# All loops written out, and both heads of a level moved together in the recurrence's inverse

## Chip, core and metric

The kernel runs on one core of one Trainium2 chip. The metric is the time of one execution in device microseconds; the kernel before takes 2701.41 us (median of 3 runs, 2699.93 to 2706.42). The engines are named as in the profile: PE (TensorE; PEld is its weight loads, PEq its sequencer), DVE (VectorE), ACT (ScalarE), POOL (GpSimd) and SP (SyncE, here only loads). A name with a q behind it (DVEq, ACTq, PEldq) stands for an engine's sequencer rows: waits, register operations, branches.

## The reference

Two decoder layers over 512 tokens of width 1024, each between two half-step SwiGLU FFNs. Layer 0 is RWKV-7 time mixing with 16 heads of 64, layer 1 is sparse attention over shared keys and values.

```python
for l in range(DEPTH):                      # DEPTH = 2
    x = x + 0.5 * swiglu(rmsnorm(x, norm_ffn1[l]), ffn1_w_gate[l], ffn1_w_up[l], ffn1_w_down[l])
    h = rmsnorm(x, norm_mix[l])
    if l < N_A:  x = x + rwkv7_time_mix(h, ...)       # layer 0
    else:        x = x + nsa_attention(h, shared, ...)  # layer 1
    x = x + 0.5 * swiglu(rmsnorm(x, norm_ffn2[l]), ffn2_w_gate[l], ffn2_w_up[l], ffn2_w_down[l])
    if l == N_A - 1:  shared = nsa_shared_kv(x, ...)
# inside rwkv7_time_mix, for every head and token:
    sa = jnp.einsum('bhij,bhj->bhi', state, -kk_t)
    state = (state * w_t[:, :, None, :] + sa[..., None] * (kk_t * a_t)[:, :, None, :]
             + v_t[..., :, None] * k_t[..., None, :])
    y = jnp.einsum('bhij,bhj->bhi', state, r_t)
```

## The kernel before

The program is a row of stages, one after another, each with its own set of semaphores and a barrier between: a transpose of x, FFN, mix_project (the RWKV projections), recurrence, project_add, FFN, shared_kv, FFN, queries, attention, project_add, FFN, and a transpose back. In every stage each engine has its own instruction list, and semaphores order them (`wait_ge` before an instruction, `then_inc` behind it). The order within a list is the order in which the code is written.

**The projections.** Float32 products are made in three passes of rounded high and low parts (`three_passes`, L146 to L152). SP loads a weight unit of 128x1024 into one of four slots, DVE splits it (`split_unit`: a CAST on L141, a subtraction on L143), PE multiplies it. In `ffn` the gate and up units of a group run in a hardware loop (`Fori`, L258, L264, L287, L331, L334, L362, L380) with four units in its body; the down units are written out. `mix_project` has such a loop for each of its projections k and v on every engine (L451) and for r on all but SP and DVE; beside the units of k, DVE makes two mixed tiles per unit (L488, L492). `attention` is a loop of two iterations (L1691, L1789, L1843, L1950) whose body holds 44 written-out steps on PE, ACT and DVE. In a loop every wait whose value depends on the iteration needs a register, which its own small instruction sets (in attention they all have line L1655).

**The recurrence** (L613 on) is written out already: it walks through 8 pairs of heads, two heads h = 0, 1 at a time, in chunks of 64 tokens. Each pair needs the inverse of a unit triangular 64x64 matrix for each of 8 chunks and both heads. It is doubled up in five levels (`LEVELS`). The factor and its transpose of head h lie in `xx[h]` (called `x[h]` and `xt[h]`). One level is, for each head: 8 small matmuls `parts @ x` into PSUM bank 6 + h ("the g matmuls", L842), a copy to `g[h]` by ACT (L1008, waits for semaphore g_mm), 16 small matmuls of `g[h]` and `xt[h]` into bank 2h ("the x matmuls", L853 and L856, wait for g), and an addition into `xx[h]` by DVE (L1166, waits for x_mm); the next level's g matmuls wait for that addition (semaphore x). The last level updates only the transpose (L1168). A small float32 matmul shows as two records in the trace. Between the g and the x matmuls of levels 0 to 3 PE does a piece of the next pair's preparation (`prepare`, parts 0 to 3); in the last pair there is none. The core of a level on DVE and on ACT:

```python
for h in range(2):                                   # DVE, L1162
    at(dve, p, "x_mm", 2 * level + h + 1)
    TT(both, bank[:, 2 * h], both, ALU.add).then_inc(s["x"], 1)
for h in range(2):                                   # ACT, L1006
    at(act, p, "g_mm", 2 * part + h + 1)
    A(g[h]..., bank[:, 6 + h, 0:NT * C], ACT.Copy).then_inc(s["g"], 1)
```

After the levels PE applies the inverse (L865, "the au matmuls", 64x128 each), ACT copies both heads (L1014), and a chain of states over the chunks follows (L901, L926, L1182).

Of the kernel before, what the change touches and what calls it, by code (L numbers as in the profile page):

```python
# [13 lines left out]
P = 128  # L14
# [164 lines left out]
class Norm:  # L179
# [37 lines left out]
    def tensor(self, pe):  # L217

        if self.first:
# [5 lines left out]
            "act32", "silu", "sq", "sq_sum", "ready"] + NORM_SEMS  # L225
# [6 lines left out]
def ffn(core, tag, x_gain, w_gate, w_up, w_down, ahead):  # L232
# [6 lines left out]
    with ExitStack() as ctx:  # L239
# [14 lines left out]
        def _(sp):  # L254
            unit = 0
            for f0, nf in groups:
                skip = 1 if f0 == 0 else 0
                with sp.Fori(0, nf // 2 - skip) as i:  # L258
# [5 lines left out]
                with sp.Fori(0, ND // 4) as i:  # L264
# [8 lines left out]
        def _(dve):  # L273
# [11 lines left out]
            for f0, nf in groups:  # L285

                with dve.Fori(0, nf // 2) as i:  # L287
# [22 lines left out]
        def _(pe):  # L310
# [4 lines left out]
            for f0, nf in groups:  # L315
# [13 lines left out]
                if f0 == 0:  # L329
                    gate_up(0, True)  # L330
                    with pe.Fori(0, nf // 2 - 1) as i:  # L331
                        gate_up(i + 1, False)
                else:
                    with pe.Fori(0, nf // 2) as i:  # L334
                        gate_up(i, False)
# [21 lines left out]
        def _(act):  # L357
# [3 lines left out]
            for f0, nf in groups:  # L361
                with act.Fori(0, nf // 2) as i:  # L362
                    for j in range(2):
# [5 lines left out]
                        act.sem_inc(s["ready"], 1)  # L369
# [5 lines left out]
        def _(pool):  # L375
# [4 lines left out]
            for f0, nf in groups:  # L380
                with pool.Fori(0, nf // 2) as i:
                    for j in range(2):
# [6 lines left out]
                        pool.sem_inc(s["ready"], 1)  # L389
# [14 lines left out]
            "dx", "mix32", "mix_hi", "mix_lo", "out", "st0", "st1", "st2", "st3", "ready", "pad"]  # L404


def mix_project(core, tag, rkv, lora):
# [21 lines left out]
    with ExitStack() as ctx:  # L429
# [13 lines left out]
        def units_of(eng, name, body, unrolled=False):  # L443
# [6 lines left out]
            elif name in MAIN:  # L450
                with eng.Fori(0, n // 4) as i:  # L451
# [23 lines left out]
        def _(dve):  # L475
            dve.sem_inc(s["w_ready"], SLOTS)
            dve.sem_inc(s["ready"], 1)

# [38 lines left out]
        def _(act):  # L517
# [5 lines left out]
            def round_tile(name, m, slot, d):  # L523
                act.wait_ge(s["mix32"], m + 1)
                act.wait_ge(s["ready"], 1)
# [31 lines left out]
        def _(pool):  # L557
# [4 lines left out]
            def low_tile(name, m, slot, d):  # L562
                pool.wait_ge(s["mix_hi"], m + 5)
                pool.wait_ge(s["ready"], 1)
# [43 lines left out]
    "score": 3, "bl": 2, "kl": 2, "nm": 2, "part": 2, "x_init": 4, "lakv": 1, "aw": 1, "g_mm": 10, "g": 10,  # L608
    "x_mm": 10, "x": 10, "au_mm": 2, "au": 2, "rp_mm": 1, "rp": 1, "f_mm": 1, "f": 1, "z_mm": 1, "z": 1, "within": 1,
# [14 lines left out]
def recurrence(core, tag, rkv, lora, yhi, ylo):  # L624
# [16 lines left out]
    with ExitStack() as ctx:  # L641
# [101 lines left out]
        def _(pe):  # L743
# [48 lines left out]
            def step(p, slot, first, last):  # L792
# [34 lines left out]
                for level in range(len(LEVELS)):  # L827
                    over = level == len(LEVELS) - 1
                    for h in range(2):
# [8 lines left out]
                        else:  # L838
                            at(pe, p, "x", 2 * (level - 1) + h + 1)
# [4 lines left out]
                        mm.then_inc(s["g_mm"], 1)  # L844
                        if level == 0 and h == 0:
                            lak_v()
                    if not last and level < 4:
                        prepare(p + 1, 1 - slot, level)
                    for h in range(2):
                        at(pe, p, "g", 2 * level + h + 1)  # L850
# [7 lines left out]
                        mm.then_inc(s["x_mm"], 1)  # L858

                at(pe, p, "aw", 1)  # L860
                for h in range(2):
                    at(pe, p, "x", 8 + h + 1)
# [79 lines left out]
        def _(act):  # L942
# [55 lines left out]
            def step(p, slot, first, last):  # L998
# [1158 lines left out]
```

## Time and profile before

| | |
|---|---|
| median of 3 runs | 2701.41 us |
| the profiled execution's own time | 2708.74 us |
| its span, first to last instruction | 2706.9 us |
| PE busy, DVE busy | 2434.5 us (90%), 1606.1 us (59%) |
| ACT busy, POOL busy | 634.9 us (23%), 563.5 us (21%) |
| mean granted PE clock | 0.948 |
| instruction fetches by PE (queue q8) | 113 packets, 1.85 MB |

The busy times are sums over stages with different limits, so they are to be read by stage. The stages begin, in us from the span's start, at 17 (FFN), 393 (mix), 598 (recurrence), 999 (project_add), 1052 (FFN), 1422 (shared_kv), 1541 (FFN), 1912 (queries), 2000 (attention), 2273 (project_add) and 2326 (FFN, to 2697).

### The profile page before, as it was taken

What the parts mean: (1) busy time and instruction counts of PE and PEld (TensorE: products, weight loads), DVE (VectorE), ACT (ScalarE), POOL (GpSimd) and SP (SyncE); (2) the same over time, 40 slices, a digit from 0 to 9 for tenths busy, and PEclk for the clock granted to TensorE, in tenths of its full rate; (3) what the DMA queues carried; (4) which work ended last, traced back from release to release, by engine and by line L of the source; (5) the groups of instructions that cost most, each with busy time, mean ns of one, the idle gap of its engine ahead of it and who ended that gap; (6) DMA issues with size and microseconds to landing.
All of it is one profiled execution on the core that took longest, in us unless ns stands there. A gap on an engine that the chain in (4) does not pass through costs nothing. (4 is left out here: it accounts for less than half of the span.)

```text
span 2706.9 us, 44357 instructions
## 1 busy us (share of the span) xinstructions
PE 2434.5 (90%) x16952; PEld 1977.2 (73%) x16952; DVE 1606.1 (59%) x2182; ACT 634.9 (23%) x1246; POOL 563.5 (21%) x382
## 2 busy tenths in 40 slices
PE   7999977987888869999999699999849898999998
PEld 6888865765666657888877588888638687788887
DVE  6646569945666545656556465656536565565654
ACT  3100012223545322101012310101435453210001
POOL 3212135421212102302030021213111300221213
PEclk9999997998999979999999799999969899999999
DMA  4333222430000012333325333332351101333331
GB/s 133 103 94 101 82 74 71 128 110 29 16 30 16 17 33 78 96 99 101 94 78 163 106 101 94 93 99 73 113 130 37 37 2 32 94 103 91 103 87 66
DMA packets 375943, 216.95 MB, mean 80 GB/s; under 512 B 18880, under 2 KB 359808, under 8 KB 375776
## 3 DMA queue, kind: packets, MB, share of 16 engines
q1 hardware_dynamic: 367648, 198.83, 26.0%
q10 hardware_dynamic: 8128, 15.83, 1.6%
q8 instruction: 113, 1.85, 0.3%
q14 instruction: 54, 0.44, 0.1%
HBM read 198.73 MB, written 15.89 MB: 79 GB/s over the span
## 5 line engine op out<-in xcount | busy, mean ns | idle before, releaser
L143 DVE TENSOR_TENSOR w_lo_ffn<-w_raw,w_hi_ffn 128x1024 fp32r<-128x1024 f32 x272 | 508.7, 1870 | 9.4
L387 POOL TENSOR_TENSOR act_ffn<-gated_ffn,usc_ffn 128x512 f32<-128x512 f32 x88 | 128.1, 1456 | 1007.4 <-ACT gated_ffn L367 1007.4
L367 ACT ACTIVATE gated_ffn<-gsc_ffn 128x512 f32<-128x512 f32 x88 | 55.8, 634 | 1010.4 <-DVE gsc_ffn L292 1010.4
L150 PE MATMUL p_gate_ffn<-hhi_ffn,w_hi_ffn 128*128 128x512 f32 x704 | 278.2, 395 | 7.6 <-DVE hlo_ffn L205 7.6
L150 PE MATMUL p_up_ffn<-hhi_ffn,w_hi_ffn 128*128 128x512 f32 x704 | 274.6, 390 | 2.9 <-DVE w_lo_ffn L143 2.9
L151 PE MATMUL p_gate_ffn<-hlo_ffn,w_hi_ffn 128*128 128x512 f32 x704 | 277.2, 394 | 0.0
L150 PE MATMUL p_down_ffn<-ahi_ffn,w_hi_ffn 128*128 128x512 f32 x704 | 274.9, 390 | 2.4 <-DVE x_res L303 2.4
L152 PE MATMUL p_gate_ffn<-hhi_ffn,w_lo_ffn 128*128 128x512 f32 x704 | 276.9, 393 | 0.0
L292 DVE TENSOR_TENSOR gsc_ffn<-p_gate_ffn,rstd_ffn 128x512 f32<-128x512 f32 x88 | 60.9, 692 | 363.6 <-PE p_up_ffn L152 363.0
L151 PE MATMUL p_up_ffn<-hlo_ffn,w_hi_ffn 128*128 128x512 f32 x704 | 274.6, 390 | 0.0
L152 PE MATMUL p_up_ffn<-hhi_ffn,w_lo_ffn 128*128 128x512 f32 x704 | 274.5, 390 | 0.0
L152 PE MATMUL p_down_ffn<-ahi_ffn,w_lo_ffn 128*128 128x512 f32 x704 | 273.9, 389 | 0.0
L151 PE MATMUL p_down_ffn<-alo_ffn,w_hi_ffn 128*128 128x512 f32 x704 | 273.9, 389 | 0.0
L141 DVE CAST w_hi_ffn<-w_raw 128x1024 fp32r<-128x1024 f32 x272 | 191.1, 702 | 29.5 <-PEq L311 29.5
L303 DVE SCALAR_TENSOR_TENSOR x_res<-p_down_ffn,x_res 128x512 f32<-128x512 f32 x96 | 66.3, 690 | 204.1 <-PE p_down_ffn L152 204.1
L390 POOL TENSOR_TENSOR alo_ffn<-act_ffn,ahi_ffn 128x512 f32 x88 | 150.6, 1712 | 98.7 <-ACT ahi_ffn L370 98.7
L150 PEld LDWEIGHTS p_gate_ffn<-hhi_ffn,w_hi_ffn 128*128 128x128 f32 x704 | 134.3, 191 | 40.7 <-DVE w_lo_ffn L143 12.3
L150 PEld LDWEIGHTS p_down_ffn<-ahi_ffn,w_hi_ffn 128*128 128x128 f32 x704 | 132.1, 188 | 34.1 <-issue 7.1
L150 PEld LDWEIGHTS p_up_ffn<-hhi_ffn,w_hi_ffn 128*128 128x128 f32 x704 | 132.6, 188 | 31.0 <-DVE w_lo_ffn L143 3.4
L151 PEld LDWEIGHTS p_gate_ffn<-hlo_ffn,w_hi_ffn 128*128 128x128 f32 x704 | 134.1, 191 | 28.3 <-issue 0.2
L152 PEld LDWEIGHTS p_gate_ffn<-hhi_ffn,w_lo_ffn 128*128 128x128 f32 x704 | 134.1, 191 | 28.2
L152 PEld LDWEIGHTS p_up_ffn<-hhi_ffn,w_lo_ffn 128*128 128x128 f32 x704 | 132.5, 188 | 27.5
(341 smaller groups left out, 4490.5 us busy)
## 6 DMA issues: line engine op xcount, KB each, us to landing
w_raw<-in_ffn_w_gate_dram SPq DMA_DIRECT2D x88, 512.0 KB, 3.8
w_raw<-in_ffn_w_up_dram SPq DMA_DIRECT2D x88, 512.0 KB, 3.8
w_raw<-in_ffn_w_down_dram SPq DMA_DIRECT2D x64, 512.0 KB, 4.1
w_raw<-in_ffn_w_down_dram SPq DMA_DIRECT2D x32, 384.0 KB, 3.4
w_raw<-in_rw_w_rkv_dram SPq DMA_DIRECT2D x24, 512.0 KB, 4.5
rkv_scratch<-staged_mix ACTq DMA_DIRECT2D x24, 256.0 KB, 2.5
w_raw<-in_kv_w_dram SPq DMA_DIRECT2D x12, 512.0 KB, 4.7
w_raw<-in_rw_w_o_dram SPq DMA_DIRECT2D x8, 512.0 KB, 5.4
```

The costliest lines, as they stand in the source:

```text
L141: nc.vector.tensor_copy(hi, raw).then_inc(s["w_hi"], 1)
L143: nc.vector.tensor_tensor(lo, raw, fp(hi), ALU.subtract).then_inc(s["w_ready"], 1)
L150: nc.tensor.matmul(out, whi, hi, start=first, stop=False)
L151: nc.tensor.matmul(out, whi, lo, start=False, stop=False)
L152: return nc.tensor.matmul(out, wlo, hi, start=False, stop=last)
L292: nc.vector.tensor_tensor(gsc[:, j], p_gate[:, j], norm.rstd[:], ALU.mult).then_inc(s["gate"], 1)
L303: nc.vector.scalar_tensor_tensor(out=core.x[:, d], in0=p_down[:, d % 2], scalar=0.5, in1=core.x[:, d], op0=ALU.mult, op1=ALU.add).then_inc ...
L367: nc.scalar.activation(gated[:], gsc[:, j], ACT.Silu).then_inc(s["silu"], 1)
L387: nc.gpsimd.tensor_tensor(act32[:], gated[:], usc[:, j], ALU.mult).then_inc(s["act32"], 1)
L390: nc.gpsimd.tensor_tensor(flat(alo[:, one(2 * i + j)]), act32[:], flat(fp(ahi[:, one(2 * i + j)])), ALU.subtract).then_inc(s["a_lo"], 1)
```

## The change

Two things. Every `Fori` becomes a Python `for`, so that all iterations stand in the instruction lists one after another, with constant addresses and wait values; the small `ready` semaphore increments that the loops had carried go too. And in the recurrence's levels the two heads share one tile each (`factors` for `xx`, `blocks` for `g`), ACT copies both heads from two banks in one instruction, DVE adds both heads from two banks in one, and the semaphores g_mm, g, x_mm and x count levels and no longer heads (5 instead of 10 per pair). Every loop is changed as the first one of this diff:

```diff
@@ ffn, and the same on every loop of mix_project, project_add and attention
-                with sp.Fori(0, nf // 2 - skip) as i:
+                for i in range(nf // 2 - skip):
@@ recurrence: tiles
-        xx = [sb(f"xx{h}", [P, 2, NT, C]) for h in range(2)]
+        factors = sb("factors", [P, 2, 2, NT, C])
+        xx = [factors[:, h] for h in range(2)]
-        g = [sb(f"g{h}", [P, NT, C]) for h in range(2)]
+        blocks = sb("blocks", [P, 2, NT, C])
+        g = [blocks[:, h] for h in range(2)]
@@ recurrence: tensor, a level
-                            at(pe, p, "x", 2 * (level - 1) + h + 1)
+                            at(pe, p, "x", level)
                         for t in range(NT):
...
-                        mm.then_inc(s["g_mm"], 1)
+                        if h == 1:
+                            mm.then_inc(s["g_mm"], 1)
                         if level == 0 and h == 0:
                             lak_v()
                     if not last and level < 4:
                         prepare(p + 1, 1 - slot, level)
+                    at(pe, p, "g", level + 1)
                     for h in range(2):
-                        at(pe, p, "g", 2 * level + h + 1)
...
-                        mm.then_inc(s["x_mm"], 1)
+                    mm.then_inc(s["x_mm"], 1)
@@ recurrence: scalar
-                        for h in range(2):
-                            at(act, p, "g_mm", 2 * part + h + 1)
-                            A(g[h][:].rearrange("p t c -> p (t c)"), bank[:, 6 + h, 0:NT * C], ACT.Copy).then_inc(s["g"], 1)
+                        at(act, p, "g_mm", part + 1)
+                        A(blocks[:].rearrange("p h t c -> p h (t c)"), bank[:, 6:8, 0:NT * C], ACT.Copy).then_inc(s["g"], 1)
@@ recurrence: vector
-                    for h in range(2):
-                        at(dve, p, "x_mm", 2 * level + h + 1)
-                        if not over:
-                            both = xx[h][:].rearrange("p a t c -> p (a t c)")
-                            TT(both, bank[:, 2 * h], both, ALU.add).then_inc(s["x"], 1)
-                        else:
-                            TT(xt[h], tiles(bank[:, 2 * h, NT * C:]), xt[h], ALU.add).then_inc(s["x"], 1)
+                    at(dve, p, "x_mm", level + 1)
+                    if not over:
+                        both = factors[:].rearrange("p h a t c -> p h (a t c)")
+                        TT(both, bank[:, 0:4:2], both, ALU.add).then_inc(s["x"], 1)
+                    else:
+                        both = factors[:, :, 1].rearrange("p h t c -> p h (t c)")
+                        TT(both, bank[:, 0:4:2, NT * C:], both, ALU.add).then_inc(s["x"], 1)
```

DVE's list before, in the recurrence, from the addition of level 0 to that of level 2 (the last word in brackets is what a row waits for; x2 is one row for each head):

```order
L1166 TENSOR_TENSOR xx_rec<-bank_rec,xx_rec 128x512 [waits x_mm_rec] x2
L1084 TENSOR_SCALAR sg_rec<-sg_rec 128x512 [waits tw_rec]
L1086 TENSOR_SCALAR sqk_rec<-bank_rec 128x512 [waits ssk_rec]
L1088 SCALAR_TENSOR_TENSOR cum_rec<-resets_rec,sg_rec 128x512 [waits sg_rec]
L1090 TENSOR_SCALAR ctr_rec<-cum_rec 128x8 [waits cum_rec]
L1166 TENSOR_TENSOR xx_rec<-bank_rec,xx_rec 128x512 [waits x_mm_rec] x2
```

The same place in the changed kernel:

```order
L1161 TENSOR_TENSOR factors_rec<-bank_rec,factors_rec 128x1024 [waits x_mm_rec]
L1080 TENSOR_SCALAR sg_rec<-sg_rec 128x512 [waits tw_rec]
L1082 TENSOR_SCALAR sqk_rec<-bank_rec 128x512 [waits ssk_rec]
L1084 SCALAR_TENSOR_TENSOR cum_rec<-resets_rec,sg_rec 128x512 [waits sg_rec]
L1086 TENSOR_SCALAR ctr_rec<-cum_rec 128x8 [waits cum_rec]
L1161 TENSOR_TENSOR factors_rec<-bank_rec,factors_rec 128x1024 [waits x_mm_rec]
```

Nothing has moved between the additions; each pair of additions of 512 elements is one of 1024, behind the matmuls of both heads.

PE's list before at the end of attention's body, which it runs twice, with the register operations of the loop:

```order
L1765 MATMUL bank_att<-ident,probs_att 128x128 x4
L1786 MATMUL bank_att<-vv_att,pt_att 128x64 x6
L1655 REGISTER_ALU x2
L1786 MATMUL bank_att<-vv_att,pt_att 128x64 x8
L1755 MATMUL bank_att<-ident,osb_att 128x128 x4
L1789 REGISTER_ALU
L1789 COMPARE_AND_BRANCH
```

The same place in the changed kernel, where the second half follows at once:

```order
L1782 MATMUL bank_att<-vv_att,pt_att 128x64 x14
L1751 MATMUL bank_att<-ident,osb_att 128x128 x4
L1729 MATMUL bank_att<-kc_att,qp_att 128x31 x4
L1738 MATMUL bank_att<-khi_att,q_att 128x128
L1739 MATMUL bank_att<-klo_att,q_att 128x128
L1740 MATMUL bank_att<-causal_att,ident_att 128x128
```

The matmuls have kept their order; the register operations and the branch are gone.

## Rows read from the trace of the kernel before

**Rows 1.** Busy time by stage: stretch, its length, then us busy (instructions) of PE, PEld, DVE, ACT, POOL; clock; DMA share; GB/s.

```profile
17.00:393.00 376.00, 364.50 (x1586) 299.48 (x1586) 228.47 (x213) 49.90 (x74) 96.97 (x60) 0.99 0.32 92
598.00:999.00 401.00, 310.46 (x7072) 241.53 (x7072) 229.68 (x410) 170.66 (x288) 65.11 (x56) 0.90 0.07 22
2000.00:2273.00 273.00, 224.74 (x1700) 197.50 (x1700) 164.08 (x550) 131.35 (x476) 32.81 (x30) 0.89 0.18 37
```

**Rows 2.** Timeline of one level of the last pair: start, length, engine, line, operation.

```profile
957.78 0.68 PE L842 MATMUL bank_rec<-xx_rec,parts_rec 64*64 64x64 f32 x16 [0.25 <-DVE xx_rec L1166]
958.29 0.28 PE L853 MATMUL bank_rec<-xx_rec,g_rec 64*64 64x64 f32 x4
...
960.19 0.68 PE L842 MATMUL bank_rec<-xx_rec,parts_rec 64*64 64x64 f32 x16
960.38 0.69 DVE L1166 TENSOR_TENSOR xx_rec<-bank_rec,xx_rec 128x512 f32<-128x512 f32 x1 [0.24 <-PE bank_rec L856]
960.92 0.38 ACT L1008 ACTIVATE g_rec<-bank_rec 128x256 f32<-128x256 f32 x1 [1.50 <-PE bank_rec L842]
961.12 0.68 PE L842 MATMUL bank_rec<-xx_rec,parts_rec 64*64 64x64 f32 x16 [0.25 <-DVE xx_rec L1166]
961.64 0.28 PE L853 MATMUL bank_rec<-xx_rec,g_rec 64*64 64x64 f32 x4
```

**Rows 3.** Nearest rows to the new instructions: all of L1168, one of L143, one of L974.

```profile
L1168 DVE TENSOR_TENSOR xx_rec<-bank_rec,xx_rec x16: 425/425/426, 659.1 to 969.7; 128x256 f32<-128x256 f32 x16
...
394.71 1.23 DVE L143 TENSOR_TENSOR w_lo_mix<-w_raw,w_hi_mix 128x1024 fp32r<-128x1024 f32 x1
...
712.50 0.60 ACT L974 ACTIVATE aw_rec<-bank_rec 128x512 f32<-128x512 f32 x1 [5.07 <-PE bank_rec L778]
```

**Rows 4.** PE's timeline through the levels of a pair with a next pair's preparation.

```profile
684.38 0.33 PE L853 MATMUL bank_rec<-xx_rec,g_rec 64*64 64x64 f32 x4
...
687.87 1.12 PE L756 MATMUL bank_rec<-sqk_rec,head_ones 128*128 128x512 f32 x2
...
690.64 0.33 PE L853 MATMUL bank_rec<-xx_rec,g_rec 64*64 64x64 f32 x4
...
695.64 0.33 PE L853 MATMUL bank_rec<-xx_rec,g_rec 64*64 64x64 f32 x4 [0.86 <-ACT g_rec L1008]
...
703.57 1.33 PE L853 MATMUL bank_rec<-xx_rec,g_rec 64*64 64x64 f32 x32
...
704.83 1.96 PE L865 MATMUL bank_rec<-aw_rec,xx_rec 64*64 64x128 f32 x32
```

**Rows 5.** The stretch of the recurrence in which the clock had fallen, columns as in rows 1.

```profile
679.40:682.90 3.50, 3.18 (x60) 3.21 (x62) 3.46 (x5) 1.16 (x3) 0.00 (x0) 0.51 0.02 5
```

**Rows 6.** Timeline and clock where attention's loop goes around.

```profile
2140.28 1.04 PE L1755 MATMUL bank_att<-ident,osb_att 128*128 128x128 f32 x4 [0.79 <-DVE osb_att L1947]
2144.66 1.91 PE L1733 MATMUL bank_att<-kc_att,qp_att 64*128 64x31 f32 x8 [3.34 <-issue]
2153.93 1.06 PE L1759 MATMUL bank_att<-ident,probs_att 128*31 128x128 f32 x4 [6.04 <-ACT probs_att L1818]
...
2153.67 0.20 ACT L1818 ACTIVATION_READ_ACCUMULATOR probs_att<-masked_att,nmax_att 128x1 f32 x1 [4.06 <-issue]
...
2140.30:2164.20 23.90, 14.52 (x59) 11.47 (x60) 6.39 (x20) 7.38 (x25) 9.87 (x10) 0.50 0.49 103
```

**Rows 7.** Branches back on PE (attention; FFN): ns min/median/max, first and last start.

```profile
L1789 PEldq COMPARE_BRANCH  x2: 76/2039/4002, 2140.4 to 2269.2; - x2
...
L334 PEldq COMPARE_BRANCH  x28: 76/208/217, 176.7 to 2655.2; - x28
```

**Rows 8.** Register operations behind attention's waits, by engine (L1655), ns as above.

```profile
L1655 PEldq ALU_OP  x298: 32/32/38, 2022.6 to 2265.9; - x149
L1655 ACTq ALU_OP  x232: 35/35/41, 2023.7 to 2265.2; - x116
```

**Rows 9.** The mix stage: DVE's register operations on L488.

```profile
L488 DVEq FUSED_REGOPS  x16: 99/99/117, 477.9 to 562.5; - x16
```

More of the change, by code:

```diff
@@ L224 @@
 FFN_SEMS = ["raw0", "raw1", "raw2", "raw3", "w_free", "w_hi", "w_ready", "gate", "gu_free", "x_done", "a_lo", "a_hi",
[L225 removed]
+            "act32", "silu", "sq", "sq_sum"] + NORM_SEMS
 def ffn_first_units(w_gate, w_up):
@@ L263, in _ @@
                 unit += 2 * nf
-                with sp.Fori(0, ND // 4) as i:
+                for i in range(ND // 4):
                     for j in range(4):
@@ L285, in _ @@
             for f0, nf in groups:
-                with dve.Fori(0, nf // 2) as i:
+                for i in range(nf // 2):
                     for j in range(2):
@@ L330, in _ @@
                     gate_up(0, True)
-                    with pe.Fori(0, nf // 2 - 1) as i:
+                    for i in range(nf // 2 - 1):
                         gate_up(i + 1, False)
                 else:
-                    with pe.Fori(0, nf // 2) as i:
+                    for i in range(nf // 2):
                         gate_up(i, False)
@@ L361, in _ @@
             for f0, nf in groups:
-                with act.Fori(0, nf // 2) as i:
+                for i in range(nf // 2):
                     for j in range(2):
@@ L380, in _ @@
             for f0, nf in groups:
-                with pool.Fori(0, nf // 2) as i:
+                for i in range(nf // 2):
                     for j in range(2):
@@ L450, in units_of @@
             elif name in MAIN:
-                with eng.Fori(0, n // 4) as i:
+                for i in range(n // 4):
                     for j in range(4):
@@ L607 @@
     "tilde": 4, "rk": 1, "bsum": 1, "bon": 1, "gp": 1, "gsb": 1, "vturn": 1, "vtok": 1, "turn": 3, "tok": 3,
-    "score": 3, "bl": 2, "kl": 2, "nm": 2, "part": 2, "x_init": 4, "lakv": 1, "aw": 1, "g_mm": 10, "g": 10,
-    "x_mm": 10, "x": 10, "au_mm": 2, "au": 2, "rp_mm": 1, "rp": 1, "f_mm": 1, "f": 1, "z_mm": 1, "z": 1, "within": 1,
+    "score": 3, "bl": 2, "kl": 2, "nm": 2, "part": 2, "x_init": 4, "lakv": 1, "aw": 1, "g_mm": 5, "g": 5,
+    "x_mm": 5, "x": 5, "au_mm": 2, "au": 2, "rp_mm": 1, "rp": 1, "f_mm": 1, "f": 1, "z_mm": 1, "z": 1, "within": 1,
     "chain": 6, "state": 6, "y_mm": 1, "ysb": 1, "mean": 1, "dev": 1, "sqy": 1, "var": 1, "lny": 1, "rs": 1,
@@ L1151, in step @@
                     at(dve, p, "nm", h + 1)
-                    both = xx[h][:].rearrange("p a t c -> p (a t) c")
+                    both = xx[h].rearrange("p a t c -> p (a t) c")
                     TT(both, both, eye, ALU.add).then_inc(s["x_init"], 1)
@@ L1223, in _ @@
             pe.sem_inc(s["w_free"], SLOTS)
-            with pe.Fori(0, ND // 4) as i:
+            for i in range(ND // 4):
                 for j in range(4):
@@ L1690, in _ @@
                 sp.dma_start(dst[:], core.consts[name]).then_inc(s["consts"], 16)
-            with sp.Fori(0, 2) as i:
+            for i in range(2):
                 for g in range(2):
@@ L1787, in weigh @@
                 mm.then_inc(s["o_mm"], 1)
-            with pe.Fori(0, 2) as i:
+            for i in range(2):
                 scores(i, 0)
@@ L1841, in copy @@
                     A(pt[:, u % 2, 1, 0:n], bank[:, 5, 0:n], ACT.Copy).then_inc(s["copied_a"], 1)
-            with act.Fori(0, 2) as i:
+            for i in range(2):
                 for u in range(U + 1):
@@ L1948, in combine @@
                                        op0=ALU.mult, op1=ALU.add).then_inc(s["o"], 1)
-            with dve.Fori(0, 2) as i:
+            for i in range(2):
                 for u in range(U + 2):
```

10 lines of the change are left out of this document (2 added, 8 removed).

## The prediction

> **What bounds the kernel now.** I read the busy times by stage first [rows 1]. The change touches three kinds of stage. In an FFN, PE is busy 364.5 of 376 us at clock 0.99, DVE 228 and ACT 50: PE alone is the bound, and a loop matters there only if it leaves PE without work. In the recurrence no engine is full: PE 310, DVE 230, ACT 171 of 401 us. Such a stage is a chain of hand-overs, and what counts is how long one link waits for the last. Attention is between: PE 225 of 273 us, clock 0.89.
>
> Then I read the timeline of one level in the last pair, where nothing else is mixed in [rows 2]. The reader is to see two heads in a staggered row. PE begins head 0's x matmuls at 958.29; head 1's g matmuls come at 961.12, and the next x matmuls at 961.64: a level lasts 3.35 us, and PE is idle for 0.25 us of it. While DVE adds head 0, PE does head 1's x matmuls; while ACT copies head 0's g, PE does head 1's g matmuls. Every addition (0.69 us) and every copy (0.38 us) has the other head's matmuls beside it.
>
> **The merged level.** What it removes is one addition and one copy per level. What it adds is that nothing of them has cover any more, except where `prepare` gives PE other work. I build the new level from T, the start of its x matmuls. PE's part does not change: the addition of head 1 began at 960.38, T + 2.09 [rows 2], and now that is where the one addition begins. Its length is not in the trace. From 256 to 512 elements the same addition goes from 0.425 us [rows 3] to 0.69, so another 512 cost about 0.53: 1.22 us; a DVE subtraction of 128x1024 took 1.23 [rows 3]. The ends are 1.2 and, if the second bank costs nothing, 0.69. It ends at T + 3.31. The g matmuls follow 0.05 later (961.12 against the addition's end at 961.07), now for both heads in one piece: 0.51 for the first (from 957.78 to 958.29 PE was done with one head) plus 0.68 for the second, to T + 4.55. The copy starts 0.05 later and takes 0.60, as another copy of 128x512 does [rows 3]; it ends at T + 5.20, and the x matmuls begin at T + 5.25. Against 3.35 that is **+1.9 us** for a level with no cover.
>
> With cover I follow one pair [rows 4].
> - Level 0 to 1: x matmuls at 684.38, preparation from 687.87 (T + 3.49) up to 690.64. PE now starts the g matmuls at T + 3.36 and not with head 1's at T + 2.83 [rows 2], and has both heads' to do behind it, so preparation starts at T + 4.45. The copy is hidden behind its 2.77 us. +0.95.
> - Level 1 to 2: PE waited 0.86 us for ACT here, which was late with table loads and two activations of the next pair. The same ACT work still ends last, and then one copy of 0.60 stands where a copy of 0.38 was enough. +0.25; if ACT's wait gave no cover, 0.95.
> - Level 2 to 3: a product of the preparation stands on PE and again covers the copy. +0.95.
> - Level 3 to 4: no preparation, +1.9 as above.
> - Level 4 to the au matmuls: x matmuls at 703.57, au at 704.83, 1.26 us later. Now both heads' x matmuls must end (T + 1.15), then one addition of 512 elements (0.69): au at T + 1.95. +0.7.
>
> That is 4.75 us for each of seven pairs, 33.3 us. In the last pair four levels go without cover, 7.6, with 0.7 at the au matmuls and 0.3 at the first copy: 8.6. Level 0's copy in the other pairs lies behind two matmuls of preparation and costs nothing; if that cover were gone it would be 0.25 a pair. Together **+41.9 us**. All that follows in the pair (au, the chain over the chunks, the next scores) waits for the inverse, so nothing takes the delay back. Bounds: if DVE's second bank were free, 0.53 less on each of 32 long additions and 0.27 on each of 8 short ones, 19 us less: +23; with no cover at level 1 to 2, +47.
>
> **The clock in the recurrence.** The mean clock of the stage is 0.90 [rows 1]; it falls once in a pair. In one such stretch of 3.5 us it stood at 0.51 and PE was busy 3.18 [rows 5]; at full clock that work takes about half, so a stretch costs up to 1.6 us. The merged levels give PE new gaps of 1.2 us (the addition) and 0.65 us (the copy). One more such stretch in every pair would be 13 us, none 0. I take **+3**, nearer the low end, since a level keeps 2.9 us of matmuls in at most 5.25.
>
> **The loops.** In attention the loop goes round once [rows 6, 7]. PE's last transposes are at 2140.28; its branch takes 4.00 us, and the next scores start after 3.34 us of idle. ACT then stops for 4.06 us in mid step, waiting for nothing that the profile shows, and PE waits 6.04 for it. Written out, PE and ACT should just go on: 3.34 + 4.06 = 7.4. The clock was 0.50 from 2140.3 to 2164.2, in part because of these gaps; the last 10 us of that stretch are PE work in a row, and I count 3 us for a clock that rises earlier. **-10.5**, ends -4 (ACT's stop alone) and -15.
>
> Between these places attention's waits need register operations: 298 on PE at 32 ns, 9.5 us in all, and 232 on ACT, 8.1 us [rows 8]. Most pass while PE still has matmuls queued; where PE has waited for a copy they stand in its way. I take half, **-5**; ends 0 and, if those of both engines were on the path, -17.6. With constant addresses SP also gets the stage's first loads out a little sooner, about **-1**, end 0.
>
> In the mix stage DVE sets the pace beside k; 16 register operations of 99 ns stand between its instructions: **-1.6** [rows 9]. End 0.
>
> In the FFNs I count 0. The branch back takes 0.2 us of PE's sequencer [rows 7], and PE's queue covers it: the matmul stream has no gap there, and PE is the bound. If that cover were gone, the 28 branches of L334 and 12 of L331 would be 8 us. DVE, ACT and POOL are never late for PE. The project_add loops are alike.
>
> [...]
>
> **Sum.** 41.9 + 3 - 10.5 - 5 - 1 - 1.6 = +26.8 us. On the profiled execution's 2708.7 that is 2735.5; it lies 7.3 us above the median of the runs, so I put the difference on the median: 2701.4 + 26.8 = **2728 us**, a ratio of 1.010.
>
> **Rivals.**
> 1. *Busy time counts, not hand-overs.* If DVE's and ACT's queues set the recurrence's pace, merging saves their fixed cost: 2 x 0.69 becomes 1.22 and 2 x 0.38 becomes 0.60, about 0.15 us each on some 40 levels, so some 12 us less instead of 41.9 more. Then the sum is -12 - 18.1 = -30, 2671 us. It decides as soon as an engine has work queued at its addition or copy. For it: level 1 to 2, where ACT is late. Against: the additions begin 0.24 us after PE's matmuls [rows 2], and 230 of 401 us on DVE [rows 1]. 8%.
> 2. *The delay is about cancelled.* A cheap second bank (+23 for the levels): 23 + 3 - 18.1 = +8; or, with the levels as forecast, all register operations of PE and ACT on attention's path (-17.6) and the upper end at its branch (-15): 41.9 + 3 - 17.6 - 15 - 2.6 = +10. With both, -6. 2695 to 2711. Against: busy PE between, and an addition that grows with its length [rows 3]. 13%.
> 3. *The clock falls with the gaps*, +13 instead of +3, or the longer lists bring stops of 4 us on PE in straight code, as ACT had one in mid step [rows 6], three of them 12 us: 2738 to 2750. 15%. [...]
> The forecast itself has 64%, with its own range of 2713 to 2738.
>
> **Numbers.** To hold 8 in 10, the range goes from 2707 (rival 2's upper part) to 2745 (most of rival 3). A measurement of this kernel tells about 0.3%, 8 us, from no change. Faster is rival 1, 8%; within 8 us is most of rival 2 and a little of the forecast's low side, 12%; slower the rest, 80%.
>
> **What would show it.** Right: the recurrence grows from 401 to about 446 us; the merged addition takes 1.2 us and begins 0.2 us after both heads' matmuls; PE's idle time before L838 and L850 grows. Attention shrinks by some 16 us, and the 3.34 and 4.06 us stops are gone. The FFN stages stay at 371 to 376 us. Wrong: additions of 0.7 us, or DVE and ACT with work queued at the levels; a stop on PE, ACT or DVE in straight code in the FFNs; a clock below 0.85 in the recurrence; or attention unchanged because PE stops at the same place to fetch.

## The result, and the profile after

The changed kernel takes 2750.34 us (median of 4 runs, 2747.16 to 2759.34) against 2700.67 for the kernel before: a ratio of 1.0177, 95% interval 1.0161 to 1.0193. That is 49.7 us more; I had forecast 26.8 more. The profiled execution took 2759.34 us, 50.6 more than the one of before.

I measured each stage from barrier to barrier in both traces (so the recurrence before counts 401.9 us here). Mix goes from 204.4 to 202.8 us, attention from 273.4 to 263.8, the four FFN stages change by 0.3 us or less, every other stage by 0.8 or less. The recurrence goes from 401.9 to 461.7. Busy time by stage in the changed kernel, the columns as in [rows 1]:

```profile
17.90:393.80 375.90, 365.04 (x1586) 300.02 (x1586) 232.07 (x213) 45.97 (x71) 93.86 (x60) 0.99 0.32 93
596.60:1058.30 461.70, 321.82 (x7072) 249.58 (x7072) 227.76 (x372) 165.28 (x248) 66.88 (x56) 0.89 0.06 19
2059.90:2323.70 263.80, 223.06 (x1700) 197.11 (x1700) 163.34 (x550) 129.80 (x475) 32.78 (x30) 0.90 0.18 38
```

Here the first thing to read is that the recurrence grew in two ways. PE's idle time (length less busy) rose from 91.4 to 139.9 us, by 48.5. But PE's busy time also rose, from 310.5 to 321.8, with the same 7072 matmuls: the same work took longer, as it does at a lower clock (the two pairs further down: 43.89 us at 0.82 and 36.24 at 1.00).

One level of the last pair, on the timeline, against [rows 2]:

```profile
1010.19 1.23 DVE L1161 TENSOR_TENSOR factors_rec<-bank_rec,factors_rec 128x1024 f32<-128x1024 f32 x1 [4.03 <-PE bank_rec L853]
...
1011.47 1.15 PE L838 MATMUL bank_rec<-factors_rec,parts_rec 64*64 64x64 f32 x32 [1.33 <-DVE factors_rec L1161]
1012.67 0.60 ACT L1004 ACTIVATE blocks_rec<-bank_rec 128x512 f32<-128x512 f32 x1 [4.14 <-PE bank_rec L838]
...
1013.32 0.33 PE L850 MATMUL bank_rec<-factors_rec,blocks_rec 64*64 64x64 f32 x4 [0.70 <-ACT blocks_rec L1004]
...
1015.45 1.23 DVE L1161 TENSOR_TENSOR factors_rec<-bank_rec,factors_rec 128x1024 f32<-128x1024 f32 x1 [4.03 <-PE bank_rec L853]
```

PE, DVE and ACT now work strictly one after another: the level repeats after 5.26 us (1010.19 to 1015.45), against 3.35. The groups by line, busy and mean, then PE's idle time before them and its releasers, say how often:

```profile
L838 PE MATMUL bank_rec<-factors_rec,parts_rec 64*64 64x64 f32 x1280 | 51.8, 232 | 63.4 <-DVE factors_rec L1161 42.5 <-issue 16.7 <-DVE parts_rec L1150 4.3
L1161 DVE TENSOR_TENSOR factors_rec<-bank_rec,factors_rec 128x1024 f32<-128x1024 f32 x32 | 39.2, 1224 | 70.1 <-PE bank_rec L853 70.1
L1004 ACT ACTIVATE blocks_rec<-bank_rec 128x512 f32<-128x512 f32 x40 | 23.9, 597 | 94.3 <-PE bank_rec L838 94.3
L862 PE MATMUL bank_rec<-aw_rec,factors_rec 64*64 64x128 f32 x256 | 19.1, 308 | 7.1 <-DVE factors_rec L1164 7.1
L908 PE MATMUL bank_rec<-bl_rec,au_rec 64*64 64x64 f32 x256 | 10.1, 221 | 7.6 <-issue 7.6
L1164 DVE TENSOR_TENSOR factors_rec<-bank_rec,factors_rec 128x512 f32<-128x512 f32 x8 | 5.5, 692 | 22.2 <-PE bank_rec L850 22.2
```

32 additions leave PE idle for 42.5 us. The row of L908 is one I had not looked for: 7.6 us of idle time with no releaser, in the middle of straight code behind the levels. On the timeline it is one stop of about 1 us in each of seven pairs (the last pair has one of 0.98 us at L898); here the third:

```profile
774.51 0.30 PE L906 MATMUL bank_rec<-kl_rec,vtok_rec 64*64 64x64 f32 x8
774.62 0.28 PE L908 MATMUL bank_rec<-bl_rec,au_rec 64*64 64x64 f32 x3
775.85 0.28 PE L908 MATMUL bank_rec<-bl_rec,au_rec 64*64 64x64 f32 x3 [0.94 <-issue]
```

The DMA records show what is on its way: PE's instructions come in packets of 16 KB on queue q8 (135 of them, 2.21 MB, before 113 and 1.85; the trace has 34605 records of PE, 256 to a packet), and one starts at 773.58. The one of the pair before it started at 722.50, with six others between. Seven packets to a pair means that their edges keep nearly the same place in every pair.

The clock's part is in two of the pairs. Both rows hold the same 884 matmuls, from one pair's first g matmul to the next one's; the second is like most pairs:

```profile
632.80:689.60 56.80, 43.89 (x884) 34.23 (x885) 25.83 (x43) 20.13 (x30) 6.86 (x6) 0.82 0.07 19
689.60:739.40 49.80, 36.24 (x884) 28.14 (x884) 28.17 (x46) 20.05 (x31) 8.58 (x7) 1.00 0.07 21
```

Where attention's loop went around [rows 6]:

```profile
2200.05 1.09 PE L1751 MATMUL bank_att<-ident,osb_att 128*128 128x128 f32 x4 [0.79 <-DVE osb_att L1942]
2201.07 1.91 PE L1729 MATMUL bank_att<-kc_att,qp_att 64*128 64x31 f32 x8
...
2205.19 1.03 PE L1755 MATMUL bank_att<-ident,probs_att 128*31 128x128 f32 x4 [0.89 <-ACT probs_att L1814]
```

The stops of 3.34 and 6.04 us are gone. From the last transposes of one half to the first of the next (a wait for `o_lo` just ahead marks these, 1.31 us before and 1.05 now) this piece takes 40.6 us instead of 50.2.

### The profile page after: what moved, and what is told of

Same layout as the page of the kernel before. It is cut to its first block and busy times, and to the rows that moved or that the text cites. A ratio compares the mean times of both kernels' runs of the same rounds, so it can differ in the third digit from the quotient of the medians.

```text
span 2757.6 us, 40748 instructions
## 1 busy us (share of the span) xinstructions
PE 2448.4 (89%) x16952; PEld 1988.7 (72%) x16952; DVE 1615.4 (59%) x2142; ACT 612.8 (22%) x1193; POOL 560.5 (20%) x382
## 3 DMA queue, kind: packets, MB, share of 16 engines
q8 instruction: 135, 2.21, 0.3%
## 5 line engine op out<-in xcount | busy, mean ns | idle before, releaser
L143 DVE TENSOR_TENSOR w_lo_ffn<-w_raw,w_hi_ffn 128x1024 fp32r<-128x1024 f32 x272 | 425.3, 1564 | 9.4
L386 POOL TENSOR_TENSOR act_ffn<-gated_ffn,usc_ffn 128x512 f32<-128x512 f32 x88 | 140.1, 1592 | 1046.3 <-ACT gated_ffn L367 1046.3
L141 DVE CAST w_hi_ffn<-w_raw 128x1024 fp32r<-128x1024 f32 x272 | 286.2, 1052 | 30.5 <-PEq L311 30.5
L151 PEld LDWEIGHTS p_up_ffn<-hlo_ffn,w_hi_ffn 128*128 128x128 f32 x704 | 132.6, 188 | 27.7
```

Source lines behind the costliest of these rows:

```text
L141: nc.vector.tensor_copy(hi, raw).then_inc(s["w_hi"], 1)
L143: nc.vector.tensor_tensor(lo, raw, fp(hi), ALU.subtract).then_inc(s["w_ready"], 1)
L151: nc.tensor.matmul(out, whi, lo, start=False, stop=False)
L386: nc.gpsimd.tensor_tensor(act32[:], gated[:], usc[:, j], ALU.mult).then_inc(s["act32"], 1)
```

## The experiments

Theory A after these readings: the merged levels cost their uncovered additions and copies (about 42 us), PE loses some 7 us more where a packet of instructions arrives late, and 11 more to the clock; the last two hang on where PE's list is cut into packets and how long the gaps are. The rivals are in the expectations. All ratios are against the kernel before on the same chip, where it took 2700.67 to 2704.6 us. The table holds what the profiles of all the kernels gave for the recurrence; "stops" are waits of PE in the dense stretch behind the levels (line 908 in the changed kernel) that have no releaser and last 0.65 us or more, about 1 us each. Shorter ones, of 0.3 to 0.6 us, stand in several kernels, three in that of before. Not counted is a wait of 2.2 us or more ahead of a pair's first g matmuls, seven in every kernel, for which the profile names no releaser either. "Shift" is the number of semaphore increments put ahead of mix_project on PE's list; they move every later packet edge.

| kernel | shift | median us | ratio (interval) | recurrence | PE busy | idle | stops |
|---|---|---|---|---|---|---|---|
| before | 0 | 2700.67 | 1 | 401.9 | 310.5 | 91.4 | 0 |
| changed | 0 | 2750.34 | 1.0177 (1.0161-1.0193) | 461.7 | 321.8 | 139.9 | 8 |
| e1 loops only | 0 | 2714.10 | 1.0043 (1.0025-1.0060) | 419.0 | 324.2 | 94.8 | 7 |
| e2 merge only | 0 | 2753.62 | 1.0194 (1.0180-1.0208) | 453.7 | 320.0 | 133.7 | 0 |
| e3 changed, filled | 0 | 2741.21 | 1.0143 (1.0126-1.0160) | 448.1 | 364.6 | 83.5 | 3 |
| e4 changed | 128 | 2745.64 | 1.0158 (1.0141-1.0174) | 456.5 | 323.0 | 133.5 | 0 |
| e5 loops only | 128 | 2697.05 | 0.9970 (0.9959-0.9981) | 401.0 | 311.4 | 89.6 | 0 |
| e6 before | 112 | 2721.24 | 1.0057 (1.0045-1.0069) | 418.7 | 322.9 | 95.8 | 8 |
| e7 changed, filled | 128 | 2739.73 | 1.0133 (1.0118-1.0148) | 448.5 | 364.9 | 83.6 | 3 |
| e8 one copy | 128 | 2704.55 | 1.0001 (0.9992-1.0009) | 411.3 | 310.1 | 101.2 | 0 |
| e9 one addition | 128 | 2727.26 | 1.0083 (1.0065-1.0101) | 431.1 | 306.0 | 125.1 | 0 |
| e10 attention only | 0 | 2698.36 | 0.9983 (0.9974-0.9993) | 400.2 | 309.5 | 90.7 | 0 |
| e11 loops only | 64 | 2704.51 | 1.0006 (0.9995-1.0017) | 408.6 | 311.2 | 97.4 | 8 |
| e12 loops only | 192 | 2699.30 | 0.9983 (0.9973-0.9993) | 407.2 | 316.6 | 90.6 | 0 |
| e13 changed | 64 | 2748.21 | 1.0171 (1.0157-1.0185) | 450.5 | 310.1 | 140.4 | 8 |
| e14 changed | 192 | 2750.19 | 1.0180 (1.0166-1.0194) | 457.3 | 323.5 | 133.8 | 0 |

**e1, the loops written out and the levels as before.** Its edit is the change's first hunk on every loop, and none of the rest.

> All loops written out, but the two heads of a level keep their own copies, additions and waits, as before the change. Theory A (the merged levels lose 4.9 us in each of eight pairs, and the lists of the recurrence lose some more by late instructions and a lower clock that both come with the longer gaps): the recurrence is 397 us long again, attention stays at 262 instead of 272 us, mix_project at 201.4 instead of 203.0, so the time is 2689 us (2683 to 2695), 11 us under the kernel before. Rival B (late instructions come from the loops written out, whatever the levels do): about 1 us of waiting with no releaser in each pair stays in the recurrence, which is then 403 to 406 us long, and the time is 2694 to 2700. Rival C (writing the loops out costs more somewhere else than attention gives back): over 2703.

Theory A missed, by 25 us. The time lies in rival C's span (over 2703), and the stops are those of rival B, with a recurrence far over its 403 to 406 us. Attention (263.9) and mix (203.0) gave what the changed kernel gave, but the recurrence, whose program is word for word that of before, took 419.0 us instead of 401.9:

```profile
596.20:1015.20 419.00, 324.23 (x7072) 249.64 (x7072) 229.74 (x412) 170.37 (x288) 65.19 (x56) 0.87 0.07 21
```

Idle time is up by 3.4, busy time by 13.7. Seven stops stand at one line, here in one pair:

```profile
711.46 0.28 PE L905 MATMUL bank_rec<-bl_rec,au_rec 64*64 64x64 f32 x3 [1.14 <-issue]
```

and behind four of the seven the clock fell. The two rows are the 10.2 us that begin 2 us behind the stops at 711.46 and 760.96; the granted clock was 0.50 in one and 1.00 in the other, and PE got through 82 matmuls in the one and 148 in the other:

```profile
713.40:723.60 10.20, 8.79 (x82) 6.09 (x82) 2.97 (x9) 2.14 (x4) 0.00 (x0) 0.50 0.01 3
...
762.90:773.10 10.20, 8.01 (x148) 5.39 (x148) 5.83 (x15) 3.95 (x6) 0.00 (x0) 1.00 0.01 3
```

**e2, the merged levels with every loop kept.**

Its edit is all hunks of the recurrence; every `Fori` stays.

> Only the merged levels, all loops kept as they were. Theory A: the recurrence is 457 us long as in the changed kernel, or a few us shorter where less of it runs at half clock, attention keeps its 272 us, so the time is 2757 us (2750 to 2764), and this kernel and the one with only the loops written out add up to the change. Rival B (the late instructions in the recurrence come from the loops written out): the recurrence is 445 to 450 us and the time 2746 to 2752. The time of a level from one head's first multiplication to the next level's should be as in the changed kernel: 7.26, 5.26, 5.54, 5.25 and 2.04 us.

2753.62, as theory A said, though the sum of parts is off: e1 is 10.3 us over the 2703.8 of before on its chip and e2 49.8, 60 together, where the change has 50. There are no stops at one line, idle time is up by 42.3, busy by 9.5. And attention is 5.6 us shorter although its loop is still there (267.8 against 273.4):

```profile
2194.32 1.91 PE L1735 MATMUL bank_att<-kc_att,qp_att 64*128 64x31 f32 x8 [3.04 <-issue]
2196.02 1.28 ACT L1820 ACT_TABLE_LOAD   x1 [3.91 <-issue]
2199.32 1.06 PE L1761 MATMUL bank_att<-ident,probs_att 128*31 128x128 f32 x4 [1.78 <-ACT probs_att L1820]
```

The kernel before has two stops of ACT there, this one at the loop's edge, beside PE's, and that of 4.06 us in mid step [rows 6]:

```profile
2146.11 1.28 ACT L1818 ACT_TABLE_LOAD   x1 [3.95 <-issue]
```

Here the stop at the edge is as long as before (3.91 us) and the one in mid step is gone: PE waits 1.78 us for ACT and not 6.04. ACT's list ahead of attention is shorter by the merged copies, and nothing else of it has changed, so whether the second stop comes hangs on the list ahead of the loop. It needs the loop as well: e6, which has the loop and ACT's list of before, has it (4.54 us), and none of the 13 kernels with attention written out has either.

**e3, filler matmuls in the gaps.**

```diff
+                def fill(n, b):
+                    for i in range(n):
+                        nc.tensor.matmul(bank[half(i % 2), b, 0:NT * C], parts[0][half(i % 2), 0, 0], ...)
...
+                    if last or level == 4:
+                        fill(2, 3)
                     at(pe, p, "g", level + 1)
...
                     mm.then_inc(s["x_mm"], 1)
+                    fill(3 if over else 5, 7)
```

> The changed kernel with filler matmuls in the gaps that the merged levels leave on TensorE: five of 64 rows by 256 columns behind the x matmuls of levels 0 to 3, three behind those of level 4, two ahead of the wait for the copy where no prepare stands there. They write banks that nothing reads then; the output is unchanged. Theory A (the two long pairs, 57 instead of 50 us, come from stretches at half clock that the gaps bring about): no stretch of the recurrence under 0.8 of the clock that comes from these gaps, all pairs 49.5 to 51 us apart, and the recurrence 440 to 450 instead of 457 us long; the time is 2735 to 2745. Rival B (the half clock has nothing to do with the gaps): the two long pairs stay and the fillers cost up to 0.2 us per level, 2750 to 2758. Rival C (the fillers delay the matmuls behind them): all pairs longer by 1 us or more, over 2758.

2741.21, 9 us less than the changed kernel, within theory A's span. But a long pair stayed (clock 0.50 to 0.57 from 769.7 to 783.3), and three stops were there: the remedy did part of what it should. The fillers have also moved PE's list and taken five of the eight stops away, so the 9 us don't show by themselves what closing the gaps does to the clock.

**e4, the changed kernel's list shifted.**

```diff
+            for _ in range(128):
+                pe.sem_inc(s["shift"], 1)
             for name, _, n in PASSES:
```

> The changed kernel with 128 semaphore increments on TensorE's list ahead of mix_project, so that every block of instructions in the recurrence begins at another place of a pair. [...] Theory A (the 1 us without a releaser in the within part of a pair, 7.6 us in seven gaps, is a block of instructions that arrives late, and where it falls is a matter of the block's edge): the gaps leave line 908 and either vanish or turn up at one other line of every pair; the recurrence changes by -6 to +6 us. Rival B (the gap belongs to the matmuls of that line): it stays at line 908 with 1.0 to 1.2 us in each pair, recurrence unchanged within 1 us. The time is 2746 to 2758 by both.

All the stops are gone and idle time is down by 6.4 us, so they go by the list's position and not by the matmuls of line 908:

```profile
L910 PE MATMUL bank_rec<-bl_rec,au_rec 64*64 64x64 f32 x256 | 8.0, 218 | 0.0
```

What ties them to the packets comes from the traces of all the kernels. In the changed kernel PE's list has 1792 records (matmuls, weight loads and what its sequencer does) from a stop to that of the next pair, for seven packets, so a packet holds 256. In the changed kernel, e1, e3, e7, e11 and e13 all 37 stops stand at the same place by this count (a remainder of 193 or 194 when the records since the start are divided by 256), and in all 45 cases, with the eight of e6, PE goes on 2.2 to 2.8 us behind the start of a packet on q8. So PE stops at the edge of a packet; that it waits for the very packet that has just started is likely, but no row names it. The time, 2745.64, is 0.4 under my span. The 128 increments take PE's sequencer from 393.2 to 412.6, one of 51 ns every 0.15 us, and PE's first product of the mix stage starts 19.8 us behind that of the sum of squares and not 10.9, yet the stage is 203.1 us long, against 202.8 in the changed kernel. Busy time did not fall (323.0).

**e5, the loops only, and shifted as e4.**

> The kernel with only the loops written out (2714.1 us, its recurrence 419.1 us long from barrier to barrier against 401.9 before, though the recurrence's own program is the same), with 128 semaphore increments on TensorE's list ahead of mix_project. Theory A (the 17 us come from where the blocks of 256 instructions end in the list: one is late by 1.1 us in the dense part of each pair, seven gaps of 7.8 us in all, and behind such a gap the granted clock halves for 10 us in every second pair): the gaps leave line 907, TensorE's busy time in the recurrence falls back from 324 to about 311 us, the recurrence is 400 to 406 us and the time 2690 to 2698 us, under the kernel before. Rival B (something else of the written-out loops slows the recurrence): it stays at 415 to 423 us and the time over 2708.

It came as theory A said: the same program with its list moved has its recurrence back at 401.0 us, and the kernel is the fastest measured.

```profile
596.70:997.70 401.00, 311.43 (x7072) 243.33 (x7072) 230.21 (x412) 170.28 (x288) 65.10 (x56) 0.90 0.07 22
```

**e6, the kernel before, with 112 increments.**

> The kernel before, loops and heads as they were, with 112 semaphore increments on TensorE's list ahead of mix_project: its blocks then end in the recurrence at about the same instruction of a pair as in the kernel with the loops written out. Theory A: seven gaps of about 1.1 us without a releaser come at the within part's matmuls, the granted clock falls in more places, and the recurrence is 412 to 422 us instead of 402; the time is 2713 to 2724 us. [...]

Moving the list makes the slow recurrence out of the fast one, with no loop written out: 418.7 us, seven stops of 1.0 us at line 913 (the same matmuls) and one of 0.9 in the last pair, busy 322.9.

```profile
597.30:1016.00 418.70, 322.88 (x7072) 248.74 (x7072) 229.81 (x412) 170.53 (x288) 64.95 (x56) 0.87 0.07 21
...
L913 PE MATMUL bank_rec<-bl_rec,au_rec 64*64 64x64 f32 x256 | 9.9, 220 | 7.0 <-issue 7.0
```

e5 and e6 together show it: e1's extra 17 us in the recurrence come from the position of PE's list, and the loops matter only because writing them out moved it.

**e7, fillers and shift.**

> The changed kernel with both remedies: the filler matmuls in the level gaps (2741.2 us by themselves, 9 under the changed kernel) and the 128 increments (2745.6 by themselves, 5 under it). If late instructions and clock are two separate costs: 2734 to 2738 us with a recurrence of 439 to 444 us, that is the 402 of before plus about 42 us of waiting in the levels less some clock that the fillers give back. If the lower clock was mostly a consequence of the late instructions: no better than the fillers alone, 2740 to 2745. Neither theory lets it come under 2725, since the waits in the levels stay.

2739.73 lies between the two spans and is hardly better than the fillers alone, but it decides nothing, since the shift did not take the stops away: three stand in both e3 and e7. The 25 fillers of a pair lengthen PE's list by 100 records, so that the packet edges no longer keep their place from pair to pair and a shift can't steer around them all.

**e8, one copy over both banks, two additions**, and **e9, one addition, two copies**, both with shift 128. Each is e5 with half of the merge:

```diff
@@ e8, scalar; g and g_mm count levels, x and x_mm heads
-                            A(g[h][:]..., bank[:, 6 + h, 0:NT * C], ACT.Copy).then_inc(s["g"], 1)
+                        A(blocks[:]..., bank[:, 6:8, 0:NT * C], ACT.Copy).then_inc(s["g"], 1)
@@ e9, vector; x and x_mm count levels, g and g_mm heads
-                            TT(both, bank[:, 2 * h], both, ALU.add).then_inc(s["x"], 1)
+                        TT(both, bank[:, 0:4:2], both, ALU.add).then_inc(s["x"], 1)
```

> All loops written out, the 128 increments, and of the merge only its half on ScalarE: one copy over both banks per level, but the additions of the two heads stay apart, each behind its own head's matmuls. By the windows of a level, the merged copy is covered by the next pair's prepare at levels 0 to 3 of seven pairs and stands bare only at level 4 of every pair and at levels 0 to 3 of the last, 12 places of 0.5 to 0.7 us: 6 to 9 us over the kernel with the loops written out and shifted (e5). The rival (the order of copies matters elsewhere too, since head 1's next multiplication now waits for a copy that started later): 15 to 20 us over it.

> All loops written out, the 128 increments, and of the merge only its half on VectorE: one addition of 1.22 us over both banks per level, but each head keeps its own copy. Theory A (the price of the merge is nearly all in the addition, whose whole 1.22 us now stands between the last x matmul and the next multiplication, 32 times, plus 8 times 0.7 us at the last level): TensorE waits at every level edge for 1.1 to 1.3 us, the recurrence is 30 to 38 us longer than the 401.0 of e5 and the time 2728 to 2736 us. With the 10 us of the merged copy (e8) that adds up to the 42 us of the whole merge. Rival B (the additions and copies cost more together than apart, since in the whole merge each waits for the other's pair): under 28 us longer, time under 2726.

Against e5, the merged copy adds 11.6 us of idle time, 7.5 us to the median, and the merged addition 35.5 us of idle time, 30.2 to the median. Together 47, and both at once (e4) 43.9 over e5: nearly additive, three quarters of it the addition. (e9's time lies 0.7 us under theory A's span, its recurrence at the lower end.) On e9's timeline the addition stands alone before PE, while the head's own copies hide:

```profile
989.06 1.23 DVE L1162 TENSOR_TENSOR factors_rec<-bank_rec,factors_rec 128x1024 f32<-128x1024 f32 x1 [3.35 <-PE bank_rec L853]
990.34 1.15 PE L839 MATMUL bank_rec<-factors_rec,parts_rec 64*64 64x64 f32 x32 [1.33 <-DVE factors_rec L1162]
991.07 0.85 ACT L1005 ACTIVATE g_rec<-bank_rec 128x256 f32<-128x256 f32 x2 [3.72 <-PE bank_rec L839]
```

Yet it has the highest mean clock of all, 0.92: busy 306.0, less than before, with 32 gaps of 1.33 us. That spoke against my reading that the merged levels' gaps bring the clock down.

**e10, only attention's two passes written out.** The kernel before with this, on SP, PE, ACT and DVE:

```diff
-            with pe.Fori(0, 2) as i:
+            for i in range(2):
```

> The kernel before with only the two passes of the attention stage written out, all other loops and the heads of a level as they were. TensorE's list up to the recurrence keeps its place, so the recurrence should stay at 401 to 403 us; the attention stage should fall from 273.4 to about 263.5, and the time be 2692 to 2697 us. If the gain in attention depended on where its lists fall rather than on the loop, it stays above 267 and the time above 2698.

The recurrence kept 400.2 us and attention fell to 263.0; the median, 2698.36, lies 1.4 above my span. The gain in attention is there whatever else is done: 262.2 to 264.0 us in all 13 kernels with its two passes written out, 273.4 and 273.0 in the two that keep the loop and ACT's list, 267.8 in e2.

**e11 and e12, the loops only, shifted by 64 and by 192.**

> The kernel with only the loops written out and 64 increments ahead of mix_project instead of 128 (none: recurrence 419.1 us; 128: 401.0). A block of instructions then ends 64 instructions earlier in a pair than with none. By theory A the recurrence's length is a matter of this place alone: somewhere from 400 to 425 us, with the same number of stops of about 1 us in each of the pairs (all or none), and the granted clock lower only where there are stops. A rival (any odd place costs, and only multiples of 128 are right) would give over 415. I expect stops at another line of the pair and 405 to 420 us, 2702 to 2716 in all.

> The same with 192 increments: a block then ends 64 instructions earlier in a pair than in e5 (128), which is 64 later than in the kernel with none. Theory A gives again a recurrence between 400 and 425 us by the place alone, with stops in all pairs or in none; I expect 401 to 412 us and 2696 to 2708 in all. The increments themselves cost nothing that mix_project shows (203.1 us with 128, 203.0 with none).

With 64 there are eight stops (9.5 us at L907 and L905), but no more busy time than in e5; with 192 none, but busy time is 5 us up. I had expected the stops of e11 at another line. L907 is e1's L905, with two lines more above it: the edge moved back by 32 matmuls, as 64 instructions should move it, and is still among those of that line. Stops and clock are thus two things: a stop need not bring the clock down, and the clock can fall without one.

**e13 and e14, the changed kernel, shifted by 64 and by 192.**

> The changed kernel with 64 increments (none: TensorE busy 321.8 us and idle 139.9 in the recurrence; 128: 323.0 and 133.5). Theory A1 (the lower clock follows from the longer gaps of the merged levels): busy stays at 319 to 325 us at every position. Theory A2 (it does not: the same work at the same gaps meets a full or a half clock by where the list's stops and the pairs happen to fall): busy comes out anywhere from 306 to 325. Idle time 133 us without late blocks and about 140 with seven of them. Time 2738 to 2755 us.

> The same with 192 increments; same readings of busy time by A1 and A2. With the loops only, 192 increments gave 407.2 us of recurrence with no stop of 1 us at one line; here I expect idle time near 134 us and, by A2, busy between 306 and 325. Time 2735 to 2750 us.

```profile
595.30:1045.80 450.50, 310.12 (x7072) 241.55 (x7072) 227.34 (x372) 165.43 (x248) 66.97 (x56) 0.91 0.06 19
...
596.50:1053.80 457.30, 323.46 (x7072) 253.00 (x7072) 227.99 (x372) 165.66 (x248) 66.62 (x56) 0.87 0.06 19
```

e14's time is 0.2 us over my span. A2 holds: with the same merged levels, busy time is 310.1 at one position and 323.5 at another. Over the four positions the merged levels cost in idle time, changed kernel less loops only, 45.1, 43.0, 43.9 and 43.2 us; that term is firm.

## Why the prediction was wrong

The direction and the largest term were right, the time lies 5 us above the range. The profiled pair grew by 50.6 us where I had 26.8. The 23.8 us between are the clock (8.3), the stops (6.4), attention's register operations (5.0) and first loads (1.0), its branch (0.9), the levels (0.2) and small differences elsewhere (2.0). By its steps:

- **The merged level, +41.9.** Right. Where there are no stops the idle time is 42.1 to 42.4 us over before (e2, e4, e14). The building blocks were right too: addition 1.224 us (1.22), copy 0.597 (0.60), level without cover 5.26 (5.25). Nothing took the delay back, so rival 1 (busy time counts) is out, and the cheap second bank of rival 2 with it.
- **No term for the place of PE's list.** This step failed. In the recurrence PE stood once in each pair, for 0.8 to 1.6 us, 7.6 us in the first seven; when the list was shifted that went away, with 6.4 us of idle time (e4). I saw ACT's stop in mid step [rows 6] and gave such stops a place in rival 3 only, as stops of 4 us. By the table's count, six of the seven packets of a pair came without a stop and the seventh with one.
- **The clock in the recurrence, +3.** This is the term that failed by most: busy time measured +11.3 us. The range of 0 to 13 that I gave was right, my choice near its low end was not. It came as two pairs of 57 us with 44 us of busy PE, where the other five of the first seven had 49.5 to 51.2 and 36 to 38. My reason for any cost (the merged levels' gaps bring the clock down) does not hold as a rule: the merged kernels show +9.5, +12.5 and +13.0, but -0.4 in e13 and, with the merged addition alone, -4.5 in e9; e1 and e6, without merged levels, show +13.7 and +12.4.
- **Attention's branch, -10.5.** Right in the sum, 9.6 us in the piece around it, with some luck in the parts: idle time fell by 8.6 us where I had 7.4, busy time by 1.0 where I had 3 for the clock (it is still at half from 2200.0 to 2213.7, 13.7 us instead of 23.9). And only part of it is a price that the loop must have: in e2 the mid-step stop of ACT is gone with the loop kept, and 5.6 us came back. What decides about that stop beyond the length of ACT's list is not shown.
- **Attention's register operations, -5, and first loads, -1.** Wrong, both about 0: the steps between last 27.98 to 28.09 us from one pair of heads to the next, against 28.05 to 28.07 and one of 28.46, and attention as a whole gained no more than the piece above. So the operations were next to nowhere on the path. SP issued the first load of `qr` 4.86 us behind the stage's first load, before 5.90, but PE's first scores from it started 19.0 us behind that load, before 19.3.
- **Mix, -1.6**, and **the FFNs, 0**: right (1.6; within 0.3 us each). Small differences in the other stages add 2.0.

So on the profiled pair: 42.1 (levels) + 6.4 (stops) + 11.3 (clock) - 9.6 (attention) - 1.6 (mix) + 2.0 (others) = 50.6 us. Rival 3, at 15%, was what came, with both its halves, though neither by the mechanism it named: the stops are eight of 1 us and go by where the list is cut, and the clock doesn't follow the gaps as a rule. In rival 2 my sum for both conditions together was wrong: from its terms it is 9 us under the kernel before, not 6. That bears on nothing above.

**What stays open** is what makes the clock fall in some pairs and not in others. The shifts moved busy time in the recurrence between 306 and 324 us without a rule that I could read off: neither the stops (e11 against e12) nor the merged gaps (e13 against e14) decide it by themselves. Falls do follow stops directly in four of seven pairs of e1, which is no proof.

## What to carry to other kernels

Here two chains that alternated on three engines covered each other's hand-overs (PE idle for 0.25 us of a level's 3.35); joining their additions into one saved 0.16 us (1.22 for two of 0.69) on an engine that had time, and put the whole instruction on the path of the one that had not: 1.33 us, 32 times. Before a change is judged by a per cent or less, its list should be moved by idle instructions, by several amounts (here 64, 128 and 192), and timed again: here position alone was worth 17 us, more than the loops (10 us), and without the shift a version 0.3% faster than before would have been thrown away as 0.4% slower. And a change should be split: the gain (attention written out) and the loss (merged levels) sat in different stages.

## What the hardware showed that I had not expected

- PE stops in straight code with no branch and nothing to wait for: in the changed kernel a 16 KB packet of instructions starts at 773.58, the matmuls break off at 774.62 and go on at 775.85.
- It does so at the edges of these packets: in six kernels all 37 stops stand at the same remainder of PE's records by 256, and with the loops written out shifts 0 and 64 gave seven or eight stops of 0.65 us and more, 128 and 192 none, alike for staggered and merged levels.
- Where attention's loop goes around, PE (3.34 us) and ACT (3.95) stop side by side. ACT's second stop, 4.06 us in mid step, is gone when its list ahead of the loop is shorter, and attention is 5.6 us shorter with it.
- The same 7072 matmuls took between 306 and 324 us of PE's time, at mean clocks of 0.92 to 0.87.
